# First product of two feed-forward stages: weights held still, 256 tokens streamed, without the transposes between

## The reference

```
# block 1: D_FF = 4096
u = rms_norm(h, g_mlp)
h = h + square(relu(u @ w_ff1)) @ w_ff2
# block 2: D_FF_2 = 2816
h2 = rmsnorm(x, norm2_w) * (1 + scale2) + shift2
x = x + gate2 * ((silu(h2 @ w_ffn_gate) * (h2 @ w_ffn_up)) @ w_ffn_down)
```

## Time and profile before

| | |
|---|---|
| median of 3 runs | 876.91 us (876.29 to 877.5) |
| the profiled execution's own time | 877.04 us |
| its span, first to last instruction | 875.4 us |
| TensorE busy | 845.4 us, 97% of the span, 3,999 matmuls |
| TensorE's weight loads busy | 704.5 us, 80% |
| VectorE busy | 588.8 us, 67% |
| ScalarE busy | 443.8 us, 51% |
| mean granted TensorE clock | 0.991 |

### The profile page before, as it was taken

How to read it: one execution, slowest core, us unless ns; L and a number is a source line. 1 busy time by engine, 2 the same in 40 slices (tenths; PEclk the granted TensorE clock), 3 DMA queues, 4 the chain that set the end, 5 groups by cost and what they waited for, 6 DMA issues and landing times.

```text
span 875.4 us, 11575 instructions
## 1 busy us (share of the span) xinstructions
PE 845.4 (97%) x3999; PEld 704.5 (80%) x3999; DVE 588.8 (67%) x902; ACT 443.8 (51%) x693; POOL 52.4 (6%) x67
## 2 busy tenths in 40 slices
PE   6999999999999999997999999999998999999996
PEld 5888888887888888875988887888887788888885
DVE  4756665867788777877766986656675746545555
ACT  6546665456444445567544436544543535434442
POOL 4000000102000000201100000011000000000000
PEclk9999999999999999999899999999999999999999
DMA  8854334688989898541565564545545365665641
GB/s 278 286 170 141 106 118 140 180 336 314 343 318 320 328 323 320 186 146 25 181 203 153 151 194 149 148 143 171 188 114 166 131 213 155 213 189 164 200 136 48
DMA packets 87621, 170.42 MB, mean 195 GB/s; under 512 B 8176, under 2 KB 32984, under 8 KB 87584
## 3 DMA queue, kind: packets, MB, share of 16 engines
q1 hardware_dynamic: 82272, 142.63, 50.7%
q0 software_dynamic: 5312, 27.30, 9.1%
HBM read 168.84 MB, written 1.05 MB: 194 GB/s over the span
## 4 chain that ended last, share of the span: by engine, by line
PE 91%; ACT 3%; DVE 2%; issue 2%; DMA 1%; POOL 0%; SPq 0%; DVEq 0%; POOLq 0%; ACTq 0%
PE B L1462 27%; PE B L1464 27%; PE B L1463 27%; PE B L1502 3%; PE B L1731 1%; ACT w_hi L536 1%; PE B L1521 1%; DMA raw<-in_w_in_dram 1%; PE B L1510 1%; PE B L1599 1%; ACT Z L579 1%; ACT junk L572 1%; PE B L1767 1%; DVE Z L971 1%; PE B L1848 1%
## 5 line engine op out<-in xcount | busy, mean ns | idle before, releaser
L1462 PE MATMUL B<-w_hi,xT_hi 128*128 128x512 f32 (+2 forms) x760 | 301.5, 397 | 1.3 <-DVE w_lo L908 1.3
L1464 PE MATMUL B<-w_hi,xT_lo 128*128 128x512 f32 (+2 forms) x760 | 294.2, 387 | 0.0
L1463 PE MATMUL B<-w_lo,xT_hi 128*128 128x512 f32 (+2 forms) x760 | 293.9, 387 | 0.0
L908 DVE TENSOR_TENSOR w_lo<-raw,w_hi 128x1024 fp32r<-128x1024 f32 (+2 forms) x156 | 186.9, 1210 | 87.8 <-ACT w_hi L536 86.4
L536 ACT ACTIVATE w_hi<-raw 128x1024 fp32r<-128x1024 f32 (+2 forms) x156 | 158.7, 1029 | 94.7 <-PE B L1464 87.9
L1464 PEld LDWEIGHTS B<-w_hi,xT_lo 128*128 128x128 f32 x760 | 144.1, 190 | 29.0
L1462 PEld LDWEIGHTS B<-w_hi,xT_hi 128*128 128x128 f32 x760 | 144.2, 190 | 28.8 <-issue 2.2
L1463 PEld LDWEIGHTS B<-w_lo,xT_hi 128*128 128x128 f32 x760 | 144.2, 190 | 26.7
L1462 PE MATMUL B<-w_hi,sT_hi 128*128 128x512 f32 x328 | 129.6, 395 | 0.0
L1464 PE MATMUL B<-w_hi,sT_lo 128*128 128x512 f32 x328 | 128.0, 390 | 0.0
L1463 PE MATMUL B<-w_lo,sT_hi 128*128 128x512 f32 x328 | 127.7, 389 | 0.0
(11 more groups left out here) (205 smaller groups left out, 698.8 us busy)
## 6 DMA issues: line engine op xcount, KB each, us to landing
raw<-in_w_in_dram SPq DMA_DIRECT2D x88, 512.0 KB, 3.7
raw<-in_w_ff_dram SPq DMA_DIRECT2D x64, 512.0 KB, 6.2
Z<-in_w_ada_dram POOLq DMA_DIRECT2D x32, 768.0 KB, 7.6
raw<-in_w_ffn_gate_dram SPq DMA_DIRECT2D x44, 256.0 KB, 3.5
raw<-in_w_ffn_up_dram SPq DMA_DIRECT2D x44, 256.0 KB, 4.1
raw<-in_w_ffn_down_dram SPq DMA_DIRECT2D x20, 512.0 KB, 4.3
raw<-in_w_mix_out_dram SPq DMA_DIRECT2D x8, 512.0 KB, 3.7
raw<-in_w_ple_gate_dram SPq DMA_DIRECT2D x8, 512.0 KB, 4.1
```

The lines of the kernel that those rows point to most:

```text
L908: nc.vector.tensor_tensor(w_lo[:, u % SPLIT, :, 0:n], raw[:, st.slot[u], :, 0:n], w_hi[:, u % SPLIT, :, 0:n].bitcast(F32), ALU.subtract).t ...
L1462: nc.tensor.matmul(bank, xh, wh, start=start, stop=False)
L1463: nc.tensor.matmul(bank, xh, wl, start=False, stop=False)
L1464: return nc.tensor.matmul(bank, xl, wh, start=False, stop=stop)
```

## The change

A new `unit_T` takes the place of `unit_pair` in both stages' first product. The weights are stationary, 128 columns of a unit at a time, and the 256 tokens move: 4 groups of columns x 2 contraction tiles x 3 = 24 matmuls of 256 columns, where `unit_pair` had 12 of 512. The result has hidden units on the partitions and tokens in the columns: two groups of 128 hidden units share a bank. So the 8 transposes of each of the 8 chunks and the 4 of each of the 11 chunks are left out. Since tokens now lie in the columns, the first stage's relu can't take 1/rms as a scale per partition; it is left out there and its square multiplies the second product's result instead (`rstd2`, two small VectorE steps ahead of the residual's update). ScalarE's relu and tanh of bank 0 wait for a new semaphore, `first_bank`, which TensorE raises when that bank is full. The first matmul of a chunk into each bank waits for the reader of the chunk before. The split into upper and lower halves reads SBUF (`nat`, `ffn_hid`) in place of the transposed banks, and ScalarE's square waits for the lower halves of the chunk before.

```diff
+            def unit_T(u, xh, xl, kt0, banks, first, last, free=None):
+                s = u % SPLIT
+                for i in range(4):
+                    bank, c0 = banks[i // 2], SEQ * (i % 2)
+                    if free is not None and i % 2 == 0:
+                        pe.wait_ge(*free[i // 2])
+                    cols = slice(i * P, (i + 1) * P)
+                    for kk in range(2):
+                        o, xk, xlk = B[:, bank, c0:c0 + SEQ], xh[:, kt0 + kk, :], xl[:, kt0 + kk, :]
+                        nc.tensor.matmul(o, w_hi[:, s, kk, cols], xk, start=first and kk == 0 and i % 2 == 0, stop=False)
+                        nc.tensor.matmul(o, w_hi[:, s, kk, cols], xlk, start=False, stop=False)
+                        m = nc.tensor.matmul(o, w_lo[:, s, kk, cols], xk, start=False, stop=last and kk == 1 and i % 2 == 1)
+                    if last and i == 1:
+                        m.then_inc(sem("first_bank"), 1)
+                m.then_inc(units_used, 1)
...
# TensorE, first stage
-                unit_pair(u, sT_hi, sT_lo, 2 * kp, (0, 1), kp == 0, kp == 3)
+                unit_T(u, sT_hi, sT_lo, 2 * kp, (0, 1), kp == 0, kp == 3)
...
-            pe.wait_ge(sem("squared"), 2)
-            hidden_T()
             with pe.Fori(1, FF_CHUNKS) as j:
                 for r in range(4):
                     pe.wait_ge(lo_done, j * 8 + (U_FFL + r - 7))
-                    unit_pair(U_FFL + r, sT_hi, sT_lo, 2 * r, (0, 1), r == 0, r == 3, 512)
+                    unit_T(U_FFL + r, sT_hi, sT_lo, 2 * r, (0, 1), r == 0, r == 3,
+                           [(sem("relu"), j * 2 - 1), (sem("relu"), j * 2)] if r == 0 else None)
                 for r in range(4):
-                    if r == 0:
-                        pe.wait_ge(sem("hid_lo"), j * 2 - 1)
+                    if r % 2 == 0:
+                        pe.wait_ge(sem("hid_lo"), j * 2 - (1 if r == 0 else 0))
                     pe.wait_ge(lo_done, j * 8 + (U_FFL + r - 3))
                     unit_wide(U_FFL + 4 + r, xT_hi, xT_lo, r, acc, False, False)
-                    if r == 1:
-                        pe.wait_ge(sem("hid_lo"), j * 2)
-                        pe.wait_ge(sem("squared"), j * 2 + 2)
-                        hidden_T()
...
# TensorE, second stage
-            pe.wait_ge(sem("ffn_hid"), 1)
-            ffn_T(0)
...
                         if e < 4:
-                            unit_pair(u, xT_hi, xT_lo, 2 * e, (0, 1), e == 0, e == 3, 512)
+                            unit_T(u, xT_hi, xT_lo, 2 * e, (0, 1), e == 0, e == 3,
+                                   [(sem("ffn_silu"), i * 2 + (half + 1)), (sem("ffn_hid"), i * 2 + (half + 1))] if e == 0 else None)
                         else:
                             unit_wide(u, sT_hi, sT_lo, 2 * half + e - 4, acc, False, False)
-                        if e == 4:
-                            pe.wait_ge(sem("ffn_hid"), i * 2 + (half + 2))
-                            ffn_T(1 - half)
...
# ScalarE, first stage
+            def relu2(j_done, chunks):
+                for b in range(2):
+                    if b == 0:
+                        act.wait_ge(sem("first_bank"), chunks)
+                    else:
+                        act.wait_ge(units_used, j_done)
+                    nc.scalar.activation(nat[:, 0, b, :], B[:, b, :], ACT.Relu).then_inc(sem("relu"), 1)
...
-                act.wait_ge(units_used, j * 8 + (U_FFL - 4))
-                relu2(j * 2 + 2)
+                relu2(j * 8 + (U_FFL - 4), j + 1)
+                act.wait_ge(sem("hid_lo"), j * 2)
+                square(j * 2 + 2)
                 for r in range(7, 7 + AHEAD):
                     loop_split(r)
-                act.wait_ge(sem("hid_T"), j * 2 + 1)
-                hidden_hi((0,))
+                hidden_hi(0, j * 2 + 1)
                 loop_split(7 + AHEAD)
-                act.wait_ge(sem("hid_T"), j * 2 + 2)
                 act.wait_ge(units_used, j * 8 + U_FFL)
-                hidden_hi((1,))
+                hidden_hi(1, j * 2 + 2)
...
# VectorE, behind the first stage
+            dve.wait_ge(sem("rstd_done"), 2)
+            link(nc.vector.tensor_tensor(rstd2, rstd[:, 1, :], rstd[:, 1, :], ALU.mult))
             dve.wait_ge(units_used, U_FFE + 4)
             for t in range(TILES):
-                add_h(t, 0, 4 + t)
+                add_h(t, 0, 4 + t, rstd2[:, t:t + 1])
...
# ScalarE and VectorE, second stage
-                nc.scalar.activation(ffn_gate[:, par, :].rearrange("p (t n) -> p t n", t=2), B[:, 0:2, 0:256], ACT.Tanh,
-                                     scale=0.5).then_inc(sem("ffn_tanh"), 1)
+                nc.scalar.activation(ffn_gate[:, par, :], B[:, 0, :], ACT.Tanh, scale=0.5).then_inc(sem("ffn_tanh"), 1)
...
-                    act.wait_ge(units_used, i * 12 + (U_FNL + 6 * half + 4))
+                    act.wait_ge(sem("first_bank"), i * 2 + (FF_CHUNKS + half + 2))
                     ffn_tanh(1 - half)
...
+                nc.vector.scalar_tensor_tensor(a, a, 1.0, B[:, 0, :], ALU.add, ALU.mult).then_inc(sem("ffn_silu"), 1)
                 dve.wait_ge(sem("ffn_silu"), count)
+                dve.wait_ge(units_used, used)
+                nc.vector.tensor_tensor(ffn_hid[:, par, :], B[:, 1, :], a, ALU.mult).then_inc(sem("ffn_hid"), 1)
```

More of the change, by code:

```diff
@@ L131 @@
     "gated": "DVE: branches times their gates", "mixed_done": "DVE: merged halves' tiles",
-    "relu": "ACT: relu tiles", "squared": "ACT: squared tiles", "hid_T": "PE: banks of transposed hidden units", "hid_hi": "ACT: upper halves",
+    "relu": "ACT: relu tiles", "squared": "ACT: squared tiles", "first_bank": "PE: first of the two banks of a chunk of hidden units", "hid_hi": "ACT: upper halves",
     "hid_lo": "DVE: lower halves", "pT_done": "PE: p transposed", "pT_hi": "ACT: upper half", "pT_lo": "DVE: lower half",
@@ L140 @@
     "mod_1": "DVE: columns of the first norm", "mod_2": "DVE: columns of the second norm", "gate_sum": "PE: gates' rows", "gate_b": "ACT: their copies",
-    "ffn_tanh": "ACT: tanh(gate / 2)", "ffn_silu": "DVE: twice silu", "ffn_hid": "DVE: twice the hidden units", "ffn_T": "PE: transposed",
-    "ffn_hi": "ACT: upper halves", "ffn_lo": "DVE: lower halves", "ffn_out": "PE: the output's banks",
+    "ffn_tanh": "ACT: tanh(gate / 2)", "ffn_silu": "DVE: twice silu", "ffn_hid": "DVE: twice the hidden units",     "ffn_hi": "ACT: upper halves", "ffn_lo": "DVE: lower halves", "ffn_out": "PE: the output's banks",
 }
@@ L309, in build @@
         nr8 = sm(2)
+        rstd2 = sm(2)
         neg_half = sm(8).rearrange("p (k t) -> p k t", t=2)
@@ L683, in _, with square, hidden_hi @@
             split_to(U_FF + 1 + AHEAD)
[L685 to L697, removed]
-            split_to(U_FF + 3 + AHEAD)
[L701 to L705, removed]
+            def relu2(j_done, chunks):
[5 more added lines that the diff above has]
+                    nc.scalar.activation(nat[:, 0, b, :], B[:, b, :], ACT.Relu).then_inc(sem("relu"), 1)
+            def square(count):
+                for b in range(2):
+                    act.wait_ge(sem("relu"), count - 1 + b)
+                    nc.scalar.activation(nat[:, 1, b, :], nat[:, 0, b, :], ACT.Square).then_inc(sem("squared"), 1)
+            def hidden_hi(b, count):
+                act.wait_ge(sem("squared"), count)
+                nc.scalar.activation(xT_hi[:, 2 * b:2 * b + 2, :], nat[:, 1, b, :].rearrange("p (k n) -> p k n", k=2),
+                                     ACT.Copy).then_inc(sem("hid_hi"), 1)
+            split_to(U_FF + 3 + AHEAD)
+            relu2(U_FF + 4, 1)
+            square(2)
+            hidden_hi(0, 1)
+            hidden_hi(1, 2)
             with act.Fori(1, FF_CHUNKS) as j:
@@ L856, in ffn_hi @@
             def ffn_hi(par, count):
-                act.wait_ge(sem("ffn_T"), count)
-                nc.scalar.activation(sT_hi[:, 2 * par:2 * par + 2, :], B[:, 2 + par, :].rearrange("p (k n) -> p k n", k=2),
+                act.wait_ge(sem("ffn_hid"), count)
+                nc.scalar.activation(sT_hi[:, 2 * par:2 * par + 2, :], ffn_hid[:, par, :].rearrange("p (k n) -> p k n", k=2),
                                      ACT.Copy).then_inc(sem("ffn_hi"), 1)
             def ffn_tanh(par):
-                nc.scalar.activation(ffn_gate[:, par, :].rearrange("p (t n) -> p t n", t=2), B[:, 0:2, 0:256], ACT.Tanh,
-                                     scale=0.5).then_inc(sem("ffn_tanh"), 1)
+                nc.scalar.activation(ffn_gate[:, par, :], B[:, 0, :], ACT.Tanh, scale=0.5).then_inc(sem("ffn_tanh"), 1)
             split_to(U_FN + 3 + FFN_AHEAD)
-            act.wait_ge(units_used, U_FN + 4)
+            act.wait_ge(sem("first_bank"), FF_CHUNKS + 1)
             ffn_tanh(0)
@@ L1402, in ffn_lo, with ffn_hidden @@
                 dve.wait_ge(sem("ffn_hi"), count)
-                nc.vector.tensor_tensor(sT_lo[:, 2 * par:2 * par + 2, :], B[:, 2 + par, :].rearrange("p (k n) -> p k n", k=2),
```

(17 more changed lines are left out.)

7 lines of the change are left out of this document (3 added, 4 removed).

## The result

The changed kernel takes 873.12 us (median of 6 runs, 872.05 to 873.81) against 877.67 us for the one before (6 runs): a ratio of 0.9948, 95% interval 0.9935 to 0.9961. It is faster by 4.6 us (3.4 to 5.7), half of the forecast 9.3 us; the forecast interval of 861.0 to 874.5 holds the time. The profiled execution fell from 877.04 to 873.29 us.

The account below looks back on a forecast made before the run. TensorE, busy 97% of the span, bounds the kernel by how densely its instructions follow. Savings of 16.0 us less 6.7 us for added weight loads give -9.3 us from 877.04, so 867.7 us; range 861.0 to 874.5.

Parts of the forecast that it names:

- 256 columns then take 120.4 - 3.4 = 117.0 ns: Step between the new first-product matmuls, read between the 264-column row (120.4 ns) and the 512-column row (226.7 ns).
- The added work: Both stages' first products: 76 units of 24 matmuls instead of 12, each 88 ns longer, adding 6.7 us.
- the upper bound of 12.9: Added us over all 76 units if 256 columns step at the 264-column row's 120.4 ns.
- 6.4, 4.9, 2.8 and 1.9 us: Savings: transposes in the first loop, transposes in the second, TensorE's wait ahead of the first loop, ahead of the second.
- The waits: Relu, silu and hidden units would be ready before TensorE's new first matmuls want them, by 0.7 us at the least.
- the edits costed at nothing: Copy and subtraction reading SBUF, the square's new wait, two small rstd steps and relu without scale: no added time.
- the 0.7 us of slack: Ahead of the transposes wanting the residual's first two updates; squaring rstd would use 0.2 us of it.
- Rival 1: Weight load sets the first products' step at 120.4 ns: -3.1 us, 873.9 us; chance 0.22.
- Rival 2: TensorE's sequencer can't feed 96 load-matmul pairs in a row; at 125 ns a step +5 us, 882 us; chance 0.05.
- Rival 3: Granted clock falls to 0.50 in the 256-column stretches: +100 us, about 968; chance 0.04.
- Rival 4: DMA loads come late, first loop's pass stays 22.67 us: -5.7 us in all, 871.3 us; chance 0.04.
- Rival 5: Weight loads don't hide behind matmuls at all, step 218 ns: +175 us, 1,052 us; chance 0.01.

Follow-up runs that it names:

- The curves: Probes of the changed kernel varying moving or stationary columns of `unit_T`; with 128 stationary, steps ran from 111.7 ns (96 moving) to 226.7 ns (512).
- The first stage alone: Only the first feed-forward stage changed, against the kernel before: 872.88 us against 877.38, ratio 0.9948.
- the second: Only the second feed-forward stage changed, against the kernel before: 877.20 us, ratio 1.0002.
- moving_curve: Changed kernel with 96, 192, 224, 240 or 288 moving columns, 128 stationary: steps 111.7 ns for 96 to 224, 112.0 for 240, 131.7 for 288.

## Why the prediction was wrong

**The mechanism was right, one term was mis-sized.** The step that failed is the one that put it: "256 columns then take 120.4 - 3.4 = 117.0 ns. I take that". Measured are 119.9 to 120.0 ns, in every one of the 19 chunks. On 1,824 matmuls that is 5.5 us, and -9.3 + 5.5 = -3.8 us is what the profiled execution did. The added work is 76 x 160 ns = 12.2 us, not 6.7, almost the upper bound of 12.9. I had drawn a line from 264 to 512 columns and read it at 256. The curves show that the part above N / 2.4 is no constant (10.0 ns at 264, 13.3 at 256, 11.6 at 288, 13.6 at 384), so a slope over 248 columns had no right to nanoseconds, and 0.1% of accuracy on 1,824 steps needs them. The row within 8 columns of the shape was the better price by far. It was even a little better than I read it: the earlier trace rows print starts to 0.01 us, which over 26 steps leaves some 0.4 ns, and in the trace each of these 26 steps is 120 ns. The upper bound is then 76 x 160 ns = 12.2 us, just what was measured. What makes up the 13.3 ns above the stream stays open.

**What was taken away came as worked out.** 6.4, 4.9, 2.8 and 1.9 us: both periods and both starts close with them. The first stage alone gave -4.5 us against -4.0 worked out with 120.0 ns, the second 0 against +0.2.

**The waits.** No relu, silu or tanh released TensorE; the edits costed at nothing cost nothing. Squaring rstd is one VectorE step, not two, of 0.15 us. The residual's update took 0.74 us a tile instead of 0.68 (it now reads a scale), and 0.3 us of the 0.7 us of slack ahead of the transposes remained.

**The rivals.** Rival 1's time, 873.9 us, is the nearest to 873.1, and I had given it 0.22. Its mechanism holds in part: with a load of 64 columns the step is 113.4 ns, with one of full width 120.0, so near the crossing neither hides all of the other; but 240 columns at 111.7 to 112.0 show that the load alone does not hold the step at 120, and the three values with 32 columns fit no account given here. Rival 2 (supply) falls: 96 even steps. Rival 3 (clock) falls at 256 columns: 1.00 in every window. It did appear where I had not asked for it: in moving_curve the 96-column stretch ran at 111.7 ns to 197.6 us and at 213 ns behind it, and a window from 199 to 202 us shows the clock at 0.50. Rival 4 (transfers) falls: the passes shortened by what the steps say at 328 GB/s. (Its sum left out the 0.35 us of the first chunk, and comes to 871.7 us, not 871.3.) Rival 5 falls: the Trainium skill's rule that loads overlap running matmuls only in other row groups ("TensorE: Matmul & The Clock Gate", part 3, the list of what overlaps) would, by the prediction's estimate, make a step of 218 ns. The same page's 256 / 2.4 + 2.5 = 109 ns (section "Back-to-back issue gap", where it stands for isolated matmuls) is 11 ns below the measured step too.

## What to carry to other kernels

Swapping the operands of a product so that its result needs no transpose doubles the matmuls if the other operand is only 256 long; count it by the step between starts, measured at just that shape, since a few nanoseconds on thousands of steps decide. Here it paid where eight transposes went for 96 matmuls and where a stall at a stage's start went, and not where four transposes went. Long streams with both halves of an operand side by side, same shapes grouped, were better than either.

## What the runs showed of the hardware

Steps between float32r matmuls in even stretches, in ns, granted clock 1.00:

| stationary columns | moving columns and step |
|---|---|
| 128 | 72, 96, 192, 224: 111.7; 240: 111.7 to 112.0; 248: 115.0; 256: 119.9; 264: 120.0; 272: 125.4; 288: 131.6; 320: 146.6; 384: 173.6; 512: 226.7 |
| 96 | 256: 116.1 |
| 64 | 128: 60.0; 192: 88.6; 256: 113.4; 288: 130.0; 384: 173.4; 512: 230.0 |
| 32 | 256: 113.5, 117.8 or 120.0 |

72 and 264 columns are from the kernel before, with tokens stationary; with more than 256 columns every matmul of a probe streamed the same columns. With 128 stationary columns the step has a floor of 111.7 ns, and with 64 it is 60.0 ns at 128 moving ones, so the floor is that of the load. The page of the Trainium skill named above puts a load at its columns over 1.2 GHz (section on LDWEIGHTS), 107 ns for 128; the trace agrees within 5 ns. From 320 to 512 columns the step grows by 0.417 ns a column, which is 1 / 2.4. Above the floor the step is this stream, N / 2.4, plus 7 to 17 ns that follow no single rule here; what makes them up stays open.
